# Loads, FFN products and padding moved across four stage boundaries of an encoder layer kernel

## The reference

```python
u = rms_norm(h, pre_mix_g)
q, k, v, rw, gates = split(u @ w_in)
att = diff_attention(q, k, v)          # 8 heads, two softmax maps each: p = p0 - lam * p1, then p @ v, rms_norm
rwk = rwkv7_bidirectional(shift_mix(rw))   # 16 heads of 64, forward and backward scans summed
merged = sigmoid(gate_a) * att + sigmoid(gate_r) * rwk
h = h + rms_norm(merged @ w_out, post_mix_g)
u = rms_norm(h, pre_ffn_g)
g, up = split(u @ w_ffn_in)            # 2 x 2816 columns
h = h + rms_norm((silu(g) * up) @ w_ffn_out, post_ffn_g)
return h[:, 16:]
```

## Time and profile before

| | |
|---|---|
| Median of three runs | 2961.85 us |
| Profiled execution, its time | 2963.58 us |
| Profiled execution, span from first to last instruction | 2961.8 us |
| TensorE busy | 96% of the span |
| VectorE, ScalarE, GpSimd busy | 47%, 33%, 21% |
| Mean granted TensorE clock | 0.983 of full speed |

### The profile page before, as it was taken

How to read it: one execution, slowest core, us unless ns; L and a number is a source line. 1 busy time by engine, 2 the same in 40 slices (tenths; PEclk the granted TensorE clock), 3 DMA queues, 4 the chain that set the end, 5 groups by cost and what they waited for, 6 DMA issues and landing times. The chain is left out here.

```text
span 2961.8 us, 44662 instructions
## 1 busy us (share of the span) xinstructions
PE 2832.0 (96%) x18476; PEld 1762.1 (59%) x18476; DVE 1382.0 (47%) x2299; ACT 982.9 (33%) x1678; POOL 631.6 (21%) x374
## 2 busy tenths in 40 slices
PE   7899999999999998899999999987999999999999
PEld 5566666666666665577777877773444444444443
DVE  3555464656555464567775655554431111112413
ACT  3323242332323241465655676673300000000001
POOL 1132231314031231100000043351143333330000
PEclk9999999999999999899999999998999999999999
DMA  3052533425243524133410567863411111103012
GB/s 95 31 179 89 160 129 107 157 75 175 73 171 95 162 103 126 60 95 83 133 32 11 122 146 181 202 200 124 141 44 43 43 50 50 43 29 142 0 36 85
DMA packets 192538, 297.73 MB, mean 101 GB/s; under 512 B 84513, under 2 KB 119105, under 8 KB 186065
## 3 DMA queue, kind: packets, MB, share of 16 engines
q1 hardware_dynamic: 181392, 252.07, 29.4%
q10 hardware_dynamic: 10944, 42.80, 3.6%
HBM read 188.54 MB, written 106.27 MB: 100 GB/s over the span
## 5 line engine op out<-in xcount | busy, mean ns | idle before, releaser
L612 PE MATMUL pp_ps<-uT,pp_w 128*128 128x347 f32 x3072 | 908.8, 456 | 3.1 <-PEq L190 2.5
L612 PEld LDWEIGHTS pp_ps<-uT,pp_w 128*128 128x128 f32 x3072 | 581.4, 190 | 319.6 <-issue 8.3
L1254 PE MATMUL at_S<-at_kR,at_qR 64*128 64x512 f32 (+1 forms) x768 | 164.1, 502 | 20.9 <-DMA at_qR<-s_kept 11.7
L1419 DVE TENSOR_REDUCE at_mn<-at_S 128x1 f32<-128x1040 f32 x128 | 156.1, 1239 | 53.0 <-PE at_S L1254 52.9
L837 POOL TENSOR_TENSOR pp_neighbours<-pp_raw 128x1040 f32<-128x1040 f32 x24 | 46.9, 1954 | 622.0 <-ACT pp_raw L713 622.0
L1313 PE MATMUL at_ob<-at_v,at_pT 128*128 128x128 f32 (+1 forms) x1152 | 174.4, 291 | 0.0
L2245 PE MATMUL fh_b<-u2T,fh_w 128*128 128x512 f32 x352 | 160.3, 598 | 2.8 <-PEq L2627 2.8
L2245 PE MATMUL fh_b<-u2T,fh_ws 128*128 128x512 f32 x352 | 158.2, 592 | 0.0
L2245 PE MATMUL fh_b<-fh_t,fh_ws 128*128 128x512 f32 x352 | 154.6, 592 | 0.0
L1313 PEld LDWEIGHTS at_ob<-at_v,at_pT 128*128 128x128 f32 (+1 forms) x1152 | 142.6, 190 | 15.4
L1254 PEld LDWEIGHTS at_S<-at_kR,at_qR 64*128 64x128 f32 x768 | 88.9, 190 | 104.9 <-issue 66.9
(11 more groups left out here) (283 smaller groups left out, 4507.3 us busy)
## 6 DMA issues: line engine op xcount, KB each, us to landing
pp_w<-in_w_main SPq DMA_DIRECT2D x64, 512.0 KB, 3.8
s_kept<-pp_ob ACTq DMA_DIRECT2D x48, 520.0 KB, 4.9
fh_w<-in_w_ffn_in SPq DMA_DIRECT2D x44, 512.0 KB, 4.5
rc_kb<-s_kb SPq DMA_DIRECT2D x64, 256.0 KB, 4.3
rc_aw<-s_ar SPq DMA_DIRECT2D x64, 256.0 KB, 4.2
s_ar<-pp_ar SPq DMA_DIRECT2D x8, 1088.0 KB, 4.0
s_kb<-pp_kb SPq DMA_DIRECT2D x8, 1088.0 KB, 7.3
s_vz<-pp_vz SPq DMA_DIRECT2D x8, 1088.0 KB, 8.6
```

The lines of the kernel that those rows point to most:

```text
L612: ins = nc.tensor.matmul(ps[s][:, n, 0:NW], weights, moving[:, n * NW:(n + 1) * NW], start=(k == 0), stop=(k == len(parts) - 1))
L1254: return nc.tensor.matmul(S[m][:, c:c + w], qR[h % 2][rows, q0:q0 + P], kR[h % 2][rows, c:c + w], start=True, stop=True)
L1419: nc.vector.tensor_reduce(mn[t % 2][:, m:m + 1], S[m][:, 0:T], AX, ALU.min).then_inc(least[m], 1)
```

## The change

Four edits in one:

1. Head 0 of the attention (k, q, v) and the lambda vectors are loaded by SyncE in the last iteration of `project_and_prepare`, after the last two weight loads, into tiles that now exist from the start of the kernel (`FirstHead`). `fr_sq` and `pp_first_part` become parts of those tiles. `attention` loads neither.
2. The ninth key block is padded to 128: vT and the first map's tiles get 112 more columns (TPAD = 1152), cleared once by GpSimd; the first transposes of values wait for that. Transposes, copies and value products of the ninth block have 128 columns or partitions.
3. Product 1 of the first two FFN tiles is made in `merge_and_mix`, between the last two `turn_out`. `ps_a` becomes two tiles of one bank each, which the FFN's product 1 uses afterwards, and the gating is two instructions. In `ffn_hidden` tile 0 begins with product 2 of tiles 0 and 1.
4. At the end of `ffn_hidden`, TensorE makes the first two of the eleven k-steps of the down product (EARLY_DOWN), in banks that the FFN's last tile no longer uses; `ffn_down` begins with the third. Four more pieces of its weights are loaded into the free buffers of the FFN weights during the last tile, and the pieces of the others are laid out anew.

```diff
+class FirstHead:
+    def __init__(self, nc, space, sems):
+        sb = lambda n, s: space.enter_context(nc.sbuf_tensor(n, s, F32))
+        self.kR, self.qR, self.vT = sb("at_kR0", [P, T]), sb("at_qR0", [P, T]), sb("at_vT", [P, TPAD])
+        self.lam_v = sb("at_lam_v", [P, 4, DQ])
+        self.here, self.lam_here = (sems.enter_context(nc.semaphore(f"at_first_{n}_here")) for n in ("head", "lam"))
+
+    def load(self, sp, kept_d, lambdas):
+        for j, x in enumerate(lambdas):
+            sp.dma_start(self.lam_v[:, j, :], x.broadcast_to([P, DQ])).then_inc(self.lam_here, 16)
+        for tile, name in ((self.kR[:], "att_k"), (self.qR[:], "att_q"), (self.vT[:, 0:T], "att_v")):
+            sp.dma_start(tile, kept_d[KEPT.index(name), 0]).then_inc(self.here, 16)
...
                     load(i, 6)
                     load(i, 7)
+                    if i == HEADS - 1:
+                        for s in range(2):
+                            sp.wait_ge(stored[s], 48 + 16)
+                        first_head.load(sp, kept_d, lambdas)
                     after(sp, "first_solved", i)
...
-                load_q_and_k(0)
-                load_v(0)
                 load_q_and_k(1)
                 stores.wait(sp)
                 load_v(1)
...
+                for tile in (vT, pr[0][0], pr[1][0]):
+                    nc.gpsimd.memset(tile[:, T:TPAD], 0.0).then_inc(tails_cleared, 1)
+                pool.wait_ge(tails_cleared, 3)
                 stores.wait(pool)
...
+                    if (h, j) == (0, 0):
+                        pe.wait_ge(tails_cleared, 3)
...
-                        k0, mk = KB[b]
-                        out = tb[0:mk, n, :] if j < 2 else beside[0:mk, 2, :]
-                        ins = nc.tensor.transpose(out, pr[t % 2][0][:, k0:k0 + mk], ident[:])
+                        out = tb[:, n, :] if j < 2 else beside[:, 2, :]
+                        ins = nc.tensor.transpose(out, pr[t % 2][0][:, b * P:b * P + P], ident[:])
...
-                        mk = KB[b][1]
-                        ins = nc.tensor.matmul(ob[:, 0:P], pT[t % 2][0:mk, b, 0:P], v[h % 2][0:mk, b, :],
+                        ins = nc.tensor.matmul(ob[:, 0:P], pT[t % 2][:, b, :], v[h % 2][:, b, :],
                                                start=(b == 0), stop=(b == NBLK - 1))
...
-                for j, x in enumerate(lambdas):
-                    act.dma_start(lam_v[:, j, :], x.broadcast_to([P, DQ])).then_inc(lam_here, 16)
-
...
+class FirstProducts:
+    def __init__(self, nc, whole):
+        self.sums = [whole.enter_context(nc.psum_tensor(f"fh_b11{b}", [P, 512], F32)) for b in range(2)]
+        self.made = whole.enter_context(nc.semaphore("fh_product1"))
+
+    def multiply(self, nc, i, wt, u2T):
+        for k in range(KH):
+            ins = nc.tensor.matmul(self.sums[i % 2][:], wt[0][i % 2][:, k, :], u2T[:, k, 0:512], start=(k == 0),
+                                   stop=(k == KH - 1), skip_group_check=True)
+        ins.then_inc(self.made, 1)
...
-                for n in range(TOK - 2, TOK):
-                    turn_out(n)
+                turn_out(TOK - 2)
+                of(pe, gated, TOK - 1)
+                of(pe, u_kept, TOK - 3)
+                for i in range(2):
+                    pe.wait_ge(w_here[i], 32)
+                    first_products.multiply(nc, i, wt, u2T)
+                turn_out(TOK - 1)
...
-                    nc.vector.scalar_tensor_tensor(ma[:], tiles(ps_a[:]), sub[:], gate[p], ALU.mult, ALU.mult).then_inc(gated, 1)
+                    for b in range(2):
+                        ks = slice(KH * b, KH * b + KH)
+                        ins = nc.vector.scalar_tensor_tensor(ma[:, ks, :], ps_a[b][:].rearrange("p (k t) -> p k t", k=KH), sub[:],
+                                                             gate[p][:, ks, :], ALU.mult, ALU.mult)
+                    ins.then_inc(gated, 1)
...
-                sp.wait_ge(down_here, 16)
+                for n in (1, 2, 4):
+                    sp.wait_ge(product[n], FT - 1)
+                sp.wait_ge(w_summed, 4 * (FT - 1))
+                for j in range(2):
+                    at = down.shape[1] + 2 * j
+                    half = wt[j][0][:].rearrange("p k x -> p (k x)").rearrange("p (k x) -> p k x", x=512)
+                    sp.dma_start(half, w_down[:, at:at + 2, 0:512]).then_inc(down_here, 16)
+                sp.wait_ge(down_here, 48)
...
-                    multiply(1, b11[b], gate[:, low, :], b_lo_lo, i)
+                        first_products.multiply(nc, i, wt, u2T)
+                    if i == 0:
+                        for early in range(2):
+                            pe.wait_ge(p1_kept, early + 1)
+                            multiply(2, b11[early], wt[0][early][:, high, :], b_hi_lo, early, start=False)
...
-                    pe.wait_ge(p1_kept, i + 1)
-                    multiply(2, b11[b], gate[:, high, :], b_hi_lo, i, start=False)
+                    if i >= 2:
+                        pe.wait_ge(p1_kept, i + 1)
+                        multiply(2, b11[b], gate[:, high, :], b_hi_lo, i, start=False)
...
+                pe.wait_ge(down_here, 16)
+                pe.wait_ge(low_made, EARLY_DOWN)
+                for made in (c21_made, c12_made, silu_1):
+                    pe.wait_ge(made, FT - 1)
+                pe.wait_ge(u2_made, FT)
+                for k in range(EARLY_DOWN):
+                    for m, out in enumerate((b4[0], b5[0], b11[0], b6)):
+                        nc.tensor.matmul(out[:], hidden[:, k, m * P:(m + 1) * P], down[:, k, :], start=(k == 0), stop=False,
+                                         skip_group_check=True)
...
-                for k in range(HALF):
+                for k in range(EARLY_DOWN, HALF):
```

More of the change, by code:

```diff
@@ L146, with front @@
 PARTS = [(0, NW - 1), (NW - 1, 2 * NW - 1), (2 * NW - 1, T)]
-def front(nc, sems, early, a, ident, ones, table, more, uT, lor, gl, gl2):
+def front(nc, sems, early, a, ident, ones, table, more, uT, lor, gl, gl2, spare):
     with ExitStack() as ctx:
@@ L2342, with ffn_down @@
 QUARTERS = TOK // 2
[L2345 removed]
+def ffn_down(nc, sems, w_down, h2_d, post_g, hidden, down, space, spare, x, y, out):
     with ExitStack() as ctx:
@@ L2647, in build @@
         stores = Stores(nc, whole)
+        lambdas = [a[n] for n in ("lq1", "lk1", "lq2", "lk2")]
+        carried = whole.enter_context(ExitStack())
+        first_head = FirstHead(nc, carried, whole)
         with fresh_semaphores(nc) as sems:
```

134 lines of the change are left out of this document (71 added, 63 removed).

## The result

The changed kernel took 2936.23 us in the median of four runs (2929.85 to 2939.54), the kernel before 2964.88 us beside it (2958.83 to 2975.29): a ratio of 0.9903, 95% interval 0.9888 to 0.9919, 28.7 us less. In a second set of runs it took 2939.18 against 2963.88, ratio 0.9915 (0.9901 to 0.9929), 24.7 us less. The forecast was 2930 with a range of 2921 to 2943, and 32.1 us less; the interval of the first ratio, 24 to 33 us less, contains that. The profiled execution took 2939.54 us, its span is 2937.6 us, the mean granted clock 0.986 (before 2961.8 and 0.983).

The account below looks back on a forecast made before the run. TensorE, busy 2832.0 of 2961.8 us, was taken as the bound, so gains come from its sequence or holes. Terms 8.65 + 12.2 + 5.5 + 5.9 = 32.25, less 0.1, gave 32.1 us and a forecast of 2930, range 2921 to 2943.

Parts of the forecast that it names:

- Part 1: Attention start: with head 0 loaded early, scores start at the boundary and the chain to the second scores moves whole, 8.65 us.
- Part 2: Attention steps: padding the ninth key block removes row-change spacing, 0.26 in 35 value steps, 0.11 in 28 plain ones, 12.2 us.
- Part 3: Mixing to FFN: first products hidden before the last transposes, less two new waits for p1 and slow clock, 5.5 us.
- Part 4: Hidden to down product: early down products remove the 3.15 hole and the slow clock behind it, leaving 0.35, 5.9 us.
- the 0.1 taken off: FFN start: VectorE's gated product split in two costs 0.1 us once, taken from the sum of 32.25.
- the bound of 7.5: Attention start: lower bound of the early-load gain, if GpSimd's large clears slow VectorE's first reductions by a us.
- the start keeps another gate: Attention start: GpSimd's clears, head 1's loads or first copies bind, half of 8.65 left, 2934 to 2935; chance 0.09.
- the bound of the plain steps: Plain attention steps: the loop of scores, minimum and exponentials becomes the bound, so TensorE could start only 0.11 us earlier.
- in a step that also transposes values ... 0.30: Attention value steps: TensorE starts 0.30 us later than the loop of scores, minimum and exponentials would allow.
- the padding brings nothing: Attention value products: spacing belongs to the fifth block's wait or the operation, not its rows; 2942 us; chance 0.17.
- that of the slow clock: Attention steps: ScalarE's loop idles TensorE, its clock falls in steady steps, 1.9 us a step, 3052 us; chance 0.03.
- the 0.45 that I had taken off: FFN start: half the difference between clock losses of 2.06 and 2.95 us, taken from 5.96 to give 5.5.

Follow-up runs that it names:

- 64 rows: Changed kernel, but the ninth key block's value products read 64 rows instead of 128, transposes and copies kept at 128; attention 411.35 us.
- quarter-scaled run: Changed kernel, but VectorE scales only 32 of the 128 columns of each attention output; attention 396.08 us, mean value step 6.33.
- part 2 undone: Changed kernel with the ninth key block back at 16 rows in transposes, copies and value products; 2947.78 us, ratio 0.9935, attention 407.29.
- both edits: Changed kernel plus tile 0's FFN product 2 made in the mixing, and the ninth block transposed with 16 columns, its value products keeping 128 rows; 2929.98 us.
- part 1 undone: Changed kernel with head 0 and the lambda vectors loaded at the attention's start again; seam before the attention 26.35 us against 18.57.
- p1 in the mixing: Changed kernel, but ScalarE copies p1 of both first FFN tiles at the end of the mixing; hidden part 536.41 us, 1.99 less.

## Why the prediction was right

The forecast of 32.1 us stands against 28.7 measured. By terms, forecast and measured between the two profiles (for part 2 between the means): part 1 8.65 and 8.2, part 2 12.2 and 8.6, part 3 5.5 and 5.9, part 4 5.9 and 5.7; 32.25 (32.1 with the 0.1 taken off) and 28.4. That 28.4 lies so near the 28.7 of the medians is partly luck, as their interval is 9 us wide and single stretches vary by more than 6. The median was missed by 6.2 us: 3.4 for the sum and 3.0 because the kernel before itself took 2964.88 beside it instead of 2961.85, less 0.2 for rounding 2929.75 up.

**Part 1** was right in its steps. Wrong in detail was that the chain from the first to the second scores moves as a whole: its value transposes run at half clock or at full, with a pitch of 1.16 or 0.90 to 0.96. That is why the seam gives 8.2 and the stretch up to the fourth step's scores 8.8. GpSimd's clears, on which the bound of 7.5 rested, did not slow the minima (1.24 us each, before and after). The rival "the start keeps another gate" fell.

**Part 2** is the term that was mis-sized. Right: rows are the cause, the size (0.28 by matmul starts against the 0.26 taken), and the bound of the plain steps (0.13 gained, 0.11 forecast). Wrong: "in a step that also transposes values ... 0.30", read as the slack of such a step. That slack was read from one loop alone. Two things stood in between. The wide ninth transpose costs up to 0.05. And the scaling by VectorE, which frees the bank of the value sums, became the next bound: it ends 1.77 behind the start of the ten value matmuls (1338.42 to 1340.19), and the next value products can follow them 0.06 later, 1.83. Before, they came 1.50 + 0.51 = 2.01 behind; with the spacing gone it would be 1.22 + 0.51 = 1.73, so 0.10 is given back. In a value step with two transposes of values the wide transpose costs only 0.02 (see 64 rows), and the step falls from 6.62 to 6.45: 0.29 - 0.10 - 0.02 = 0.17. In the mean of all value steps it is 0.15. With the measured steps, 35 x 0.15 + 26 x 0.13 = 8.6; the forecast had 35 x 0.26. The quarter-scaled run gives back 0.09 a value step, 3.0 of the 3.6 us missed. The rival "the padding brings nothing" fell with part 2 undone, and that of the slow clock too: beside TensorE's new idle of tenths of a us the granted clock is 1.00 from 1215 to 1580.

On the two pages of the Trainium skill weighed there: the loads are as long with 16 or 64 rows (0.18 us) as with 128 (0.19), as TensorE: Matmul & The Clock Gate, section LDWEIGHTS, has it, and yet the rows cost time. The 64-row run agrees with what the Trainium skill says in TensorEngine Tiling (Array Packing), section Key Properties, that a change of tiling mode drains the engine: the weight loads stand 0.20 us further apart at each change. That this spacing is a drain, no record here shows.

**Part 3** came out as worked out, both waits included (3.55 and 1.16 for 3.4 and 1.15). It gained 0.4 more: the 0.45 that I had taken off for a slower clock was not lost, since the clock cost 1.77 at its start, less than the 2.06 of before.

**Part 4** came out at 5.7. Its first half, the hole of 3.15, is firm. Its second, the slow matmuls, is worth 1.8 to 2.95, as the run without it shows; the forecast took the one value that the trace of before had.

What stays open: why the recurrence, and the stages up to the start of the projection's last small products (1175.25 to 1181.99 over the twelve profiles), vary by 6.5 and 6.7 us between executions. That is more than the error of any term. The clock is a part of it: between 1700 and 1950 us, in windows of 50, it is granted at 0.97, 0.97, 1.00, 0.95 and 0.95 in the profile after, whose recurrence is the longest, and at 1.00 in all five in the second, whose recurrence is the shortest. It can't be all: summed over windows of 2 us (an estimate from their granted clocks), the recurrence spends 13.6 to 13.7 us at half clock both where it takes 394.00 (both edits) and where it takes 398.85 (part 1 undone).

## What to carry to other kernels

When an edit takes time out of an engine's sequence, list every loop that closes over the place, not only the one that was last: here each PSUM bank that is read by another engine before it is overwritten is such a loop, and its slack (2.01 - 1.83 = 0.18 us) was smaller than the gain. A short row count in one block of a product costs at both changes, with 64 rows as with 16, so pad the rows of the product, but leave its transpose narrow. And fill the stretch beside a stage boundary to make the hole small, for the slow matmuls behind a hole of some 3 us cost another 1.8 to 2.95. No length is safe by these runs: the clock stayed through the one hole of 1.74 and fell with those of 2.99 and more, but once, at the attention's end, also behind one of 1.45.

## What the runs showed of the hardware

A change of the row count between two matmuls sets their weight loads 0.20 us further apart, equally for 16 and for 64 rows against 128, and it shows in no record but as spacing; of the two changes' 0.40, 0.28 to 0.29 is lost between the matmuls' starts. Behind a group of scores, a transpose of 128 columns holds back the next one by 0.05 us more than one of 16 (0.16 against 0.11); behind another transpose it doesn't (0.11 both).

The same hole does not always cost the same. With a hole of 3.15 us the clock fell 2.1 us into it in one kernel and a us behind its end in another (16.85 and 15.67 us for 32 matmuls). Behind the attention's hole of 1.45 us it fell in the profile after (2.34 us for ten value matmuls) and not in the second profile of the same kernel (1.28). A window over the same value transposes at the attention's start, first of the changed kernel, then of that with p1 in the mixing:

```profile
1189.00:1191.00 2.00, 1.38 (x4) 0.58 (x4) 0.00 (x0) 0.47 (x2) 2.00 (x1) 0.50 0.00 0
```

```profile
1189.00:1191.00 2.00, 1.07 (x5) 0.56 (x5) 0.00 (x0) 0.74 (x2) 2.00 (x1) 0.93 0.00 0
```

Up to here the two kernels have the same instructions. The clock came back in one (0.93) and stayed at half in the other (0.50). Where it had come back it fell again afterwards, so that the second and third steps' scores were slow (3.99 and 2.56); in the other these took 3.74 and 2.08, and the clock was back for good by 1199. To the fourth step's scores the two differ by 0.4 us only.
